# Two of the first modulation's units are halved between VectorE and TensorE

## The reference

```python
def _modulation(c, ada_w, ada_b):
    mod = jax.nn.silu(c) @ ada_w + ada_b          # (1024) @ (1024, 3072)
    shift, scale, gate = jnp.split(mod[:, None, :], 3, axis=-1)
    return shift, scale, gate
...
    shift, scale, gate = _modulation(c, ada_w[i], ada_b[i])
    h = _rmsnorm(x, norm_g[i]) * (1.0 + scale) + shift
    y = _diff_attention(h, positions, w_in0, ...)     # proj = h @ w_in first
    x = x + gate * y
```

## Time and profile before

| | before |
|---|---|
| median of 3 runs | 1538.32 us (1538.28 to 1540.69) |
| the profiled execution | 1538.38 us |
| its span, first to last instruction | 1536.5 us |
| TensorE busy | 1382.3 us, 90% of the span |
| VectorE busy | 684.7 us, 45% |
| ScalarE busy | 356.0 us, 23% |
| the chain that ended last, by engine | PE 69%, DMA 15%, DVE 9% |

### The profile page before, as it was taken

The page is one execution under the profiler, slowest core; times in us unless marked ns, Lnnn a source line. Parts: engine busy times, 40 slices in busy tenths (PEclk is TensorE's granted clock), DMA queues, the critical chain, the costliest instruction groups (busy, mean ns, idle before and its releaser), DMA issues.

```text
span 1536.5 us, 17675 instructions
## 1 busy us (share of the span) xinstructions
PE 1382.3 (90%) x6712; PEld 699.3 (46%) x6712; DVE 684.7 (45%) x1313; ACT 356.0 (23%) x778; POOL 111.6 (7%) x227
## 2 busy tenths in 40 slices
PE   4999999999999999999999989979996968769685
PEld 2444444555464444664644445455443324223242
DVE  4675524884266723332599845263121112111125
ACT  2433204653220253431500154110000000000001
POOL 4000000010100000000200000112000001000003
PEclk9999999999999999999999989989998989989898
DMA  9763136004176741003424123169999999999995
GB/s 341 261 245 125 55 110 127 4 1 164 52 254 224 237 164 56 1 1 110 148 99 161 58 110 156 64 236 396 419 410 418 420 415 417 416 418 423 423 425 238
DMA packets 85133, 338.08 MB, mean 220 GB/s; under 512 B 10343, under 2 KB 16280, under 8 KB 72376
## 3 DMA queue, kind: packets, MB, share of 16 engines
q1 hardware_dynamic: 70752, 307.24, 51.5%
q0 software_dynamic: 5664, 13.70, 3.2%
q10 hardware_dynamic: 8632, 15.99, 2.9%
HBM read 323.34 MB, written 17.24 MB: 222 GB/s over the span
## 4 chain that ended last, share of the span: by engine, by line
PE 69%; DMA 15%; DVE 9%; issue 2%; ACT 2%; POOL 1%; DVEq 0%; SPq 0%; ACTq 0%; POOLq 0%
PE score_banks L723 14%; PE bank L734 13%; DMA slots<-in_w_exp_up 12%; PE score_banks L1214 9%; PE score_banks L734 5%; PE bank L1241 5%; PE bank L707 3%; PE bank L941 3%; PE score_banks L1228 2%; PE bank L896 2%; PE bank L1043 2%; PE score_banks L1034 2%; DVE bufD L2050 2%; PE score_banks L953 1%; PE bank L957 1%
## 5 line engine op out<-in xcount | busy, mean ns | idle before, releaser
L723 PE MATMUL score_banks<-slots 128*128 128x512 f32 (+1 forms) x584 | 243.3, 574 | 3.0 <-PE score_banks L723 1.5
L1214 PE MATMUL score_banks<-slots,norm_row 128*64 128x512 f32 (+1 forms) x672 | 147.2, 607 | 42.4 <-DMA slots<-in_w_exp_up 42.2
L734 PE MATMUL bank<-slots 128*128 128x512 f32 x416 | 183.2, 594 | 2.2 <-PE bank L734 0.9
L723 PEld LDWEIGHTS score_banks<-slots 128*128 128x128 f32 x584 | 110.4, 191 | 129.6 <-issue 126.8
L2540 DVE TENSOR_TENSOR mix<-probsT,score_banks 128x256 f32<-128x256 f32 (+1 forms) x39 | 14.4, 370 | 287.7 <-ACT probsT L1688 287.7
L1241 PE MATMUL bank<-slots,mix 128*64 128x512 f32 (+1 forms) x864 | 115.2, 477 | 12.0 <-issue 9.5
L734 PEld LDWEIGHTS bank<-slots 128*128 128x128 f32 x416 | 77.5, 190 | 96.6 <-issue 95.0
L1688 ACT ACTIVATE probsT<-score_banks 128x256 f32<-128x256 f32 (+1 forms) x39 | 13.4, 343 | 436.9 <-PE score_banks L1214 376.5
L1214 PEld LDWEIGHTS score_banks<-slots,norm_row 128*64 128x64 f32 (+1 forms) x672 | 49.9, 142 | 133.9 <-issue 132.5
L734 PE MATMUL score_banks<-slots 128*128 128x512 f32 (+1 forms) x256 | 95.2, 527 | 0.3 <-PE score_banks L734 0.3
L2427 DVE SCALAR_TENSOR_TENSOR bufD<-slots,col,bufD 128x512 f32<-128x512 f32 x120 | 80.5, 746 | 0.4
(11 more groups left out here) (376 smaller groups left out, 1767.4 us busy)
## 6 DMA issues: line engine op xcount, KB each, us to landing
slots<-in_w_exp_down SPq DMA_DIRECT2D x32, 2048.0 KB, 35.6
slots<-in_w_exp_gate SPq DMA_DIRECT2D x32, 2048.0 KB, 29.5
slots<-in_w_exp_up SPq DMA_DIRECT2D x32, 2048.0 KB, 34.7
slots<-in_w_in SPq DMA_DIRECT2D x16, 2048.0 KB, 9.0
slots<-in_w_mod SPq DMA_DIRECT2D x24, 1024.0 KB, 5.2
slots<-in_ada_w SPq DMA_DIRECT2D x18, 1024.0 KB, 6.4
slots<-in_w_out SPq DMA_DIRECT2D x6, 2048.0 KB, 8.2
slots<-in_ada_w SPq DMA_DIRECT2D x3, 2048.0 KB, 20.5
```

Source lines behind the costliest of these rows:

```text
L723: last = mm(bank[:, cols], w[:, k, lo:lo + P], src[:, k, cols], start=(k == 0), stop=(k == kts - 1))
L734: last = mm(bank[:, 0:cols], features_k[:, t * P:(t + 1) * P], rhs(k), start=(k == 0), stop=(k == kts - 1))
L1214: last = mm(out, rows[:, k, :], e_gu[it.p][:, :, k, c * pc.ff:(c + 1) * pc.ff], start=(k == 0), stop=(k == KT - 1))
```

## The change

Units 1 and 3 are each halved over the contraction. VectorE weighs four of the eight blocks as before, and `reduce_columns` sums the accumulator. The other four blocks go to TensorE in the new `half_unit`: for each of the four column groups j and each block k a 128 by 128 piece of the unit is the weights and one column of silu(c) moves, so that the sum over k builds up in PSUM, already one column for each 128 features. That is 16 matmuls for a half unit. Both halves land in one bank, columns 4 to 7 and 0 to 3, and `take_halves` on VectorE adds them with the bias. `row_unit`, the copy on ScalarE and the six matmuls of the first `stay_warm` are gone.

```diff
+            def half_unit(bank, rows, first):
                 for j in range(4):
+                    for k in range(4):
+                        last = mm(bank[:, j:j + 1], rows[:, k, j * P:(j + 1) * P], silu_c[:, first + k:first + k + 1],
+                                  start=(k == 0), stop=(k == 3))
+                return last
...
-            reduce_columns()
-            row_unit()
+            bank0, bank1 = dve_banks.claim(pe), dve_banks.claim(pe)
+            pe.wait_ge(silu_ready, 1)
+            pe.wait_ge(w_in[1], unit_arrival(1))
+            half_unit(bank1, unit_view(1)[:, 4:8], 4)
+            reduce_columns(bank0)
+            reduce_columns(bank1, 4)
             pe.wait_ge(xn_ready, TT)
...
-            reduce_columns()
-            stay_warm(6)
-            reduce_columns()
+            bank2, bank3 = dve_banks.claim(pe), dve_banks.claim(pe)
+            pe.wait_ge(mod_in[0], 16)
+            half_unit(bank3, mod_half[0], 0).then_inc(mod_used, 1)
+            reduce_columns(bank2)
+            reduce_columns(bank3, 4)
             stay_warm(13)
...
+            def take_halves(n, layer, u, bias_col):
+                bank = dve_banks.take(dve)
+                part = mods[layer][:, 4 * u:4 * u + 4]
+                chain(v.tensor_tensor(part, bank[:, 0:4], col1[:, bias_col + 4 * u:bias_col + 4 * u + 4], ALU.add))
+                v.tensor_tensor(part, bank[:, 4:8], part, ALU.add).then_inc(dve_freed, 1)
...
-            weigh_unit(0)
+            weigh_first_unit()
             dve.sem_inc(unit_used, 1)
+            weigh_second_unit()
             scale_x(0)
             dve.wait_ge(act_freed, 1)
             take_columns(0, 0, 0, R1["ada_b0"])
-            weigh_unit(2)
-            take_columns(1, 0, 1, R1["ada_b0"])
-            dve.sem_inc(unit_used, 2)
-            weigh(3)
...
+            weigh_third_unit(second_unit_done)
+            dve.sem_inc(unit_used, 1)
+            weigh_fourth_unit()
             take_columns(2, 0, 2, R1["ada_b0"])
-            take_columns(3, 0, 3, R1["ada_b0"])
+            take_halves(3, 0, 3, R1["ada_b0"])
+            dve.wait_ge(mod_used, 1)
+            dve.sem_inc(mod_used, 1)
             affine(0, R1["norm_g0"], col1)
```

More of the change, by code:

```diff
@@ L283, in mod_acc @@
             return buf[:, lo + n % 2 * W:lo + (n % 2 + 1) * W]
-        def summed(n):
-            return n if n > 0 else 1
         def c_loads():
@@ L327, in fused_kernel @@
         mod_in = [sem(f"mod_half_loaded{i}") for i in range(2)]
-        row_copied = sem("second_unit_row_copied")
         mod_used, mod_summed, mod_reduced = sem("mod_half_used"), sem("mod_unit_summed"), sem("mod_unit_reduced")
@@ L684, in every_8th, with reduce_columns @@
                 return row.rearrange("p (q k) -> p k q", k=KT)[:, k, :]
-            def reduce_columns():
+            def reduce_columns(bank=None, at=0):
                 n = reduced[0]
-                pe.wait_ge(mod_summed, summed(n))
-                bank = dve_banks.claim(pe)
+                pe.wait_ge(mod_summed, n + 1)
+                bank = dve_banks.claim(pe) if bank is None else bank
                 for j in range(4):
-                    last = mm(bank[:, j:j + 1], mod_acc(n)[:, j * P:(j + 1) * P], ones[:, 0:1], start=True, stop=True)
+                    last = mm(bank[:, at + j:at + j + 1], mod_acc(n)[:, j * P:(j + 1) * P], ones[:, 0:1], start=True, stop=True)
                 last.then_inc(dve_filled, 1)
@@ L833, in out_tile @@
                 return run
[L835 to L844, removed]
+            def half_unit(bank, rows, first):
                 for j in range(4):
-                    last = mm(bank[:, j:j + 1], mod_acc(1)[0:1, j * P:(j + 1) * P], ones[0:1, 0:1], start=True, stop=True)
-                last.then_inc(dve_filled, 1)
-                reduced[0] += 1
+                    for k in range(4):
+                        last = mm(bank[:, j:j + 1], rows[:, k, j * P:(j + 1) * P], silu_c[:, first + k:first + k + 1],
+                                  start=(k == 0), stop=(k == 3))
+                return last
             def stay_warm(n):
@@ L1475, in _ @@
             table_column(col1, R1_ROWS)
[L1476 to L1479, removed]
             for k in range(KT):
@@ L2043, in _, with weigh_rows, weigh_first_unit, weigh_second_unit @@
             sums_done, halves_done = [0], [0]
-            def weigh_rows(n, k, w):
+            def weigh_rows(n, k, w, first=0):
                 c = silu_c[:, (0 if n < 12 else 8) + k:(0 if n < 12 else 8) + k + 1]
                 acc = mod_acc(n)
-                if k == 0:
+                if k == first:
                     return v.tensor_scalar(acc, w, c, None, ALU.mult)
                 return v.scalar_tensor_tensor(out=acc, in0=w, scalar=c, in1=acc, op0=ALU.mult, op1=ALU.add)
[L2052 to L2056, removed]
+            def weigh_first_unit():
+                dve.wait_ge(w_in[0], unit_arrival(0))
                 for k in range(KT):
-                    chain(weigh_rows(n, k, unit_view(n)[:, k, :]))
+                    chain(weigh_rows(0, k, unit_view(0)[:, k, :]))
                 dve.sem_inc(mod_summed, 1)
+            def weigh_second_unit():
+                dve.wait_ge(w_in[1], unit_arrival(1))
+                for k in range(4):
+                    chain(weigh_rows(1, k, unit_view(1)[:, k, :]))
+                dve.sem_inc(mod_summed, 1)
+            def weigh_third_unit(halfway):
+                dve.wait_ge(w_in[2], unit_arrival(2))
+                dve.wait_ge(mod_reduced, 1)
+                for k in range(KT):
+                    if k == 4:
+                        halfway()
+                    chain(weigh_rows(2, k, unit_view(2)[:, k, :]))
+                dve.sem_inc(mod_summed, 1)
+            def weigh_fourth_unit():
+                dve.wait_ge(mod_in[1], 16)
+                dve.wait_ge(mod_reduced, 2)
+                for k in range(4, KT):
+                    chain(weigh_rows(3, k, mod_half[1][:, k - 4, :], first=4))
+                dve.sem_inc(mod_summed, 1)
+                halves_done[0] = 2
             def weigh_half(n, half):
@@ L2083, in take_columns @@
                                 ALU.add).then_inc(dve_freed, 1)
+                dve.wait_ge(dve_freed, dve_banks.n)
+                dve.sem_inc(mod_reduced, 1)
+            def take_halves(n, layer, u, bias_col):
[3 more added lines that the diff above has]
+                v.tensor_tensor(part, bank[:, 4:8], part, ALU.add).then_inc(dve_freed, 1)
                 dve.wait_ge(dve_freed, dve_banks.n)
@@ L2183, in _, with second_unit_done @@
             take_columns(0, 0, 0, R1["ada_b0"])
-            weigh_unit(2)
-            take_columns(1, 0, 1, R1["ada_b0"])
-            dve.sem_inc(unit_used, 2)
-            weigh(3)
+            def second_unit_done():
+                take_halves(1, 0, 1, R1["ada_b0"])
+                dve.sem_inc(unit_used, 1)
+            weigh_third_unit(second_unit_done)
+            dve.sem_inc(unit_used, 1)
+            weigh_fourth_unit()
             take_columns(2, 0, 2, R1["ada_b0"])
-            take_columns(3, 0, 3, R1["ada_b0"])
+            take_halves(3, 0, 3, R1["ada_b0"])
+            dve.wait_ge(mod_used, 1)
+            dve.sem_inc(mod_used, 1)
             affine(0, R1["norm_g0"], col1)
```

## The result

| | before | changed |
|---|---|---|
| median of 20 runs | 1536.99 us (1534.68 to 1540.69) | 1541.57 us (1537.97 to 1547.58) |
| ratio of the times | | 1.0034, 95% interval 1.0025 to 1.0044 |
| profiled execution (its span) | 1538.38 us (1536.5) | 1539.24 us (1537.4) |
| start of `win0` in it | 45.85 us | 47.86 us |

The change makes the kernel slower by 0.34%; the medians are 4.6 us apart, where +3.6 was forecast. The profiled execution of the changed kernel is the second quickest of its 20, so it shows the mechanism better than the size. One execution of the kernel before, among those that e9 and e10 are compared with, took 6667 us and is left out of their ratios.

A forecast was written before the change was run, and what follows sets the result against it. It took the waits up to `win0`'s start as the bound, VectorE the long pole before, TensorE's slow clock delaying it after. `win0` moves from 45.85 to 49.5: 1538.38 + 3.6 = 1542.0 us, range 1540.3 to 1544.4.

The forecast's parts named there:

- +3.6: Start of `win0` and whole time: 3.6 us later, taken between the ends +1.95 and +6.0; chance 0.62.
- Lower clock for unit 1's half, 7.0 us: TensorE at the start: unit 1's half runs at 1.2 GHz, 22.1 to 29.1 us.
- Unit 2 starts at 31.35 after VectorE's wait: VectorE waits for unit 0's sum, queued behind the half unit; unit 2 starts at 31.35, not 27.49, losing 3.9 us.
- The transposes raise the clock, end at 38.5: TensorE's transposes from 32.6 us: they bring 2.4 GHz at 37.4 and end at 38.5.
- The rival in which they do not: Transposes leave TensorE at the lower clock until `stay_warm`: +8.1 to +10.4, or 1547.6 us; chance 0.18.
- One-column records raise it: Rival: in unit 1's half they bring the higher pace at 26.9; 1.75 us earlier, 1536.6 us; chance 0.20.
- The clock falls at 42.1 behind the transposes, so both last sums are slow: TensorE's one-column records after the transposes lose the clock at 42.1; the sums end at 45.5, not 43.8.
- `stay_warm` comes back soon enough not to bind: Ahead of `win0`: the clock returns in `stay_warm`'s 26 records; if it stayed low, 6.3 us instead of 3.15.
- its lower end of +1.95: Last two sums at the higher clock, ending at 43.8; `win0` starts at 47.8.
- its ends (+1.95 and +6.0): `win0`: last sums at the higher clock give +1.95; slow sums and `stay_warm` at the lower clock give +6.0.
- The 1542.0 us named: Whole kernel: the profiled execution's 1538.38 us before the change, plus 3.6.
- Costed at nothing: Charged no time: the copy gone from ScalarE, and the loads, with unit 1 landing at 22.1 us.

The follow-up runs named there:

- e9: e7 with the half units moving one column again instead of 120; ratio 1.0016 to the kernel before.
- e10: The changed kernel without the last thirteen matmuls of `stay_warm`; ratio 1.0038 to the kernel before.
- e1: The changed kernel with half units moving 120 equal columns of silu(c) instead of one; 1536.52 us, ratio 1.0000 to the kernel before.
- e3: The changed kernel with five 512-column matmuls of x run ahead of the table's transpose, results not read; ratio 0.9999 to the kernel before.
- e7: The changed kernel with e1, e2 and e3 together, and `stay_warm(8)` between the last two sums; 1534.55 us, ratio 0.9982 to the kernel before.
- e2: The changed kernel with unit 0's sum put ahead of unit 1's half on TensorE; ratio 1.0022 to the kernel before.
- e6: Only unit 3 halved, unit 1 left as the row unit of the kernel before; ratio 1.0035 to the kernel before.
- e5: The changed kernel with unit 3 whole on VectorE and `stay_warm(6)` between the last two sums, only unit 1 halved; ratio 1.0052 to the kernel before.

## Why the prediction came out

The forecast's cause, TensorE at 1.2 GHz in and behind the half units, is shown by e1, e3 and the pair e7 and e9. The size came out well in part by luck, as the last steps show. By its own steps, in the changed kernel's profile:

- *Lower clock for unit 1's half, 7.0 us*: 6.96, and 3.55 for the two sums behind it (forecast 3.5). Right, and shown by e1 and e3: other columns or an earlier clock take it away.
- *Unit 2 starts at 31.35 after VectorE's wait*: 31.52 after 3.15 us. Right as an event. e2 shows that it is not what sets the end, which the sum did have, since TensorE's own list ended later than VectorE's.
- *The transposes raise the clock, end at 38.5*: 5.55 us, end near 38.1, the higher pace from 36.4 on (forecast 37.4). The rival in which they do not is out, and with it, for this kernel, the rule of the Trainium skill (TensorE: Matmul & The Clock Gate, Part 4) that transposes do not count for the clock.
- *One-column records raise it*: out. They ran 10 us from 22.36 without a pause and the pace stayed at 0.22 us a record, and in e3, e6 and e9 the clock fell in or behind them. The Trainium skill's sentence (the same title, Part 1) on time under way does not hold for such records here.
- *The clock falls at 42.1 behind the transposes, so both last sums are slow*: it fell between 43.2 and 43.4, and the sums took 1.94 us together, not 3.5. The forecast had it too early by a microsecond, so h was there at 44.33 + 2.93 = 47.3, not 49.5. In e6 the forecast's path did happen, with 3.55 us for the two sums.
- *`stay_warm` comes back soon enough not to bind*: wrong. It took 4.76 us and ended last, at about 47.9, 0.6 us behind h. The same holds in all eight profiles in which `stay_warm` ran at least partly at 1.2 GHz behind the last sum: it ended 0.6 us (here and e1) to 2 us (e5) behind h.

So `win0` came at +2.0 in the profile, and the forecast's +3.6 was not reached there by either of its two steps at the end: the slow sums that it charged did not come, and the slow `stay_warm` that it charged nothing for did. That the +2.0 equals its lower end of +1.95 is luck, since that end had both fast. The medians lie 4.6 us apart, between its ends (+1.95 and +6.0). The 1542.0 us named is closer to the 1541.57 measured than the shift is, and that is luck too: it was counted from 1538.38, and the median of 20 runs of the kernel before is 1536.99, so a start 1.4 us too high covers a shift 1.0 us too small.

The two terms that were mis-sized are the last sums (3.5 charged, 1.94 measured) and `stay_warm` (nothing charged, 0.6 us in this profile, up to 2 us in others). What makes the median 4.6 and not 2.0 stays open. The clock's falling and rising at other places, as in the profiles of e2, e5, e6 and e9, is a likely part of it, and of the 9.6 us between the quickest and the slowest run of the changed kernel, but no run here shows it for one and the same kernel, and the stretch behind `win0` scatters by several us as well.

Costed at nothing and rightly so: the loads. Unit 1 landed at 22.2 (forecast 22.1), and up to `win0` no row of TensorE or VectorE waits for a later load.

## What to carry to other kernels

- In these runs a product with one moving column ran at 1.2 GHz where it came first (32 records in 6.96 us), and where it came at 2.4 GHz the clock fell in or behind it (e3, e6, e9), though PE was busy all the time. When a list gets a long run of such records, look up the pace of the nearest like row, and price what stands behind it, fillers such as `stay_warm` too, at the lower clock as well.
- Where each record loads 128 weights anyway, wide moving operands cost next to nothing more: 32 records took 3.73 to 3.81 us with 120 columns (e1, e7) and 3.63 with one (e3), all at 2.4 GHz. A broadcast can be moved and one column of the result used.
- Work moved from the bounding engine to an idle one pays only if the idle engine stays idle enough. Here its list had the transposes and sums that the bounding engine waits for, so the moved work has to be checked against what is queued behind it.

## What was not expected of the hardware

A full TensorE can be at half clock: busy 6.20 of 6.20 us up to 43.2, granted 0.50 right after, and busy 3.20 of 3.20 in that. So in these profiles a busy share of 100% does not tell the clock. And the column of the granted clock stands at 1.00 in the first 36 us of the changed kernel too, while the records' pace there was that of 1.2 GHz (6.96 us for 32 of them); there the pace has to be read instead.
